# Gate and up products by halves of the input channels, expert weights reloaded piece by piece, and the last block's inner columns taken ahead of the late one-hots

## The reference

```python
h = rms_norm(x, norm2_g)
# 4 groups of 8 experts; every token picks one group and its 2 best experts in it
xb = h_pad[buf_tok].reshape(n_blocks, MOE_BLOCK, D)      # rows gathered by expert
def expert_block(args):
    x_b, e = args
    hid = jax.nn.silu(x_b @ w_gate[e]) * (x_b @ w_up[e])  # 1024 -> 512 channels
    return hid @ w_down[e]                                # 512 -> 1024
y = einsum('tkd,tk->td', y_assign, gates)                 # two results of a token, weighted
x = rms_norm(x + y, final_g)
```

## Time and profile before

| what | value |
| --- | --- |
| median of 3 runs | 965.87 us (964.38 to 966.78) |
| the profiled execution's own time | 967.03 us |
| its span, first to last instruction | 964.9 us |
| PE busy | 857.3 us, 89% of the span |
| DVE busy | 430.1 us, 45% |
| mean granted TensorE clock | 0.948 of full speed |
| HBM read and written | 247.52 MB and 27.08 MB |

### The profile page before, as it was taken

One profiled execution on the slowest core, in us unless ns is written; L12 is line 12 of the kernel. 1 busy time (PEld: TensorE's weight loads), 2 busy tenths in 40 slices (PEclk: granted clock), 3 DMA queues, 4 the chain that ended last, 5 costly groups with the idle time before them and its releaser, 6 DMA issues.

```text
span 964.9 us, 15627 instructions
## 1 busy us (share of the span) xinstructions
PE 857.3 (89%) x5808; PEld 578.9 (60%) x5809; DVE 430.1 (45%) x622; ACT 249.0 (26%) x486; POOL 157.5 (16%) x286
## 2 busy tenths in 40 slices
PE   3989999999779994699999988898889999899965
PEld 2879978778468883555555545453445555455532
DVE  5499979848977434422222221111121222212276
ACT  5214274563745222011111111111011111111112
POOL 4100000000011000222222221111111222121162
PEclk9989999999979995599999999999899999999988
DMA  7444435221183737499999999999999999999454
GB/s 199 121 121 117 155 144 184 61 71 44 32 265 141 303 133 311 176 368 401 393 399 400 399 405 403 413 404 415 399 412 396 391 408 390 400 401 349 159 201 130
DMA packets 80890, 265.75 MB, mean 275 GB/s; under 512 B 18092, under 2 KB 43948, under 8 KB 56280
## 3 DMA queue, kind: packets, MB, share of 16 engines
q1 hardware_dynamic: 63232, 245.10, 66.6%
q0 software_dynamic: 7808, 18.54, 5.5%
q10 hardware_dynamic: 9816, 1.66, 0.9%
HBM read 247.52 MB, written 27.08 MB: 285 GB/s over the span
## 4 chain that ended last, share of the span: by engine, by line
PE 59%; SPq 17%; DMA 11%; DVE 7%; issue 3%; ACT 1%; ACTq 0%; POOL 0%; POOLq 0%; DVEq 0%
SPq L723 17%; PE ps L1203 14%; PE ps L1001 12%; DMA ring<-in_w_up 10%; PE ps L1236 7%; PE ps L1123 7%; PE ps L997 4%; PE ps L1206 2%; PE ps L1194 2%; DVE big L1583 2%; PE ps L1020 1%; PE ps L1215 1%; PE ps L1050 1%; PE ps L1029 1%; PE ps L1266 1%
## 5 line engine op out<-in xcount | busy, mean ns | idle before, releaser
L1206 PE MATMUL ps<-ring,big 128*64 128x256 f32 x896 | 211.5, 395 | 21.5 <-DMA ring<-in_w_up 21.3
L1203 PE MATMUL ps<-ring,big 128*64 128x256 f32 x896 | 214.3, 395 | 4.8 <-DMA ring<-in_w_gate 3.6
L1203 PEld LDWEIGHTS ps<-ring,big 128*64 128x64 f32 x896 | 125.5, 142 | 66.7 <-issue 18.8
L1206 PEld LDWEIGHTS ps<-ring,big 128*64 128x64 f32 x896 | 126.3, 143 | 51.9 <-DMA ring<-in_w_up 29.0
L1829 DVE TENSOR_TENSOR big<-ps,big 64x256 f32<-64x256 f32 x78 | 33.1, 426 | 267.1 <-ACT big L1480 267.0
L1001 PE MATMUL ps<-hT,w_split 128*128 128x512 f32 (+1 forms) x768 | 145.2, 344 | 4.1 <-DVE hT L1539 3.6
L1001 PEld LDWEIGHTS ps<-hT,w_split 128*128 128x128 f32 x768 | 118.0, 190 | 25.6 <-issue 11.3
L1583 DVE SCALAR_TENSOR_TENSOR big<-big,vec 128x783 f32<-128x783 f32 x116 | 119.6, 1031 | 3.0
L1480 ACT ACTIVATE big<-ps 64x256 f32<-64x256 f32 x78 | 29.3, 375 | 292.4 <-PE ps L1206 292.4
L1236 PE MATMUL ps<-ring,big 128*64 128x512 f32 x224 | 103.2, 604 | 0.0
L1237 PE MATMUL ps<-ring,big 128*64 128x512 f32 x224 | 103.2, 604 | 0.0
(11 more groups left out here) (213 smaller groups left out, 1121.8 us busy)
## 6 DMA issues: line engine op xcount, KB each, us to landing
ring<-in_w_gate SPq DMA_DIRECT2D x44, 1024.0 KB, 28.1
ring<-in_w_up SPq DMA_DIRECT2D x44, 1024.0 KB, 29.1
ring<-in_w_down SPq DMA_DIRECT2D x44, 1024.0 KB, 29.2
big<-in_w_gate SPq DMA_DIRECT2D x20, 1024.0 KB, 28.7
big<-in_w_up SPq DMA_DIRECT2D x20, 1024.0 KB, 29.8
big<-in_w_down SPq DMA_DIRECT2D x20, 1024.0 KB, 29.5
w_raw<-in_w_in SPq DMA_DIRECT2D x20, 512.0 KB, 4.0
results<-spare POOLq DMA_DIRECT2D x12, 512.0 KB, 2.9
```

Of the source, the lines that this page charges most:

```text
L1203: pe.matmul(ps[0:BLK, 6 * h, 0:FH], xT[:, k, :], gate_w[s][:, k, fs], start=(k == 0), stop=(k == KD - 1))
L1206: mm = pe.matmul(ps[BLK:2 * BLK, 6 * h + 1, 0:FH], xT[:, k, :], up_w[s][:, k, fs], start=(k == 0), stop=(k == KD - 1))
```

## The change

It has four parts.

1. `gate_up` takes a further argument q, the half of the input channels. A block now runs q = 0 for both halves h of the inner columns, and then q = 1 for both. The number of matmuls and what they sum are as before. A new semaphore, `gu_half`, is raised after q = 0, h = 1.
2. `load_expert` waits on `gu_half` ahead of the first two pieces (gate and up of the first channel half), on `gu_done[1]` ahead of the next two, and on `y_done` ahead of down, as before.
3. In DVE's tail `hidden(last)` stands ahead of the late one-hots. `result(last)` follows these, and all four `with_stored` come behind it.
4. The semaphores of the two norm vectors become one, counted to 16 and 32.

```diff
+            def load_some(e, s, first, end):
+                for l in list(in_order(s))[first:end]:
                     load(e, *l)
 ...
                 end = sp.value_load(table[0:1, bass.ds(e + (2 * E - SLOTS), 1)], min_val=1, max_val=MAXB)
+                sp.wait_ge(gu_half, end)
+                load_some(e, s, 0, 2)
                 sp.wait_ge(gu_done[1], end)
-                load_gate_up(e, s)
+                load_some(e, s, 2, 4)
                 sp.wait_ge(y_done, end)
-                load_down(e, s)
+                load_some(e, s, 4, 6)
...
-            def gate_up(b, s, target, h):
+            def gate_up(s, target, q, h):
 
                 fs = slice(h * FH, (h + 1) * FH)
-                for k in range(KD):
+                for k in range(q * KD // 2, (q + 1) * KD // 2):
                     if h == 0 and k % (KD // 2) == 0:
-                        pe.wait_ge(gate_in[s][k // (KD // 2)], target)
+                        pe.wait_ge(gate_in[s][q], target)
...
-                mm.then_inc(gu_done[h], 1)
+                if q:
+                    mm.then_inc(gu_done[h], 1)
+                elif h:
+                    mm.then_inc(gu_half, 1)
...
-                gate_up(b, s, target, 0)
-                gate_up(b, s, target, 1)
+                for q in range(2):
+                    for h in range(2):
+                        gate_up(s, target, q, h)
...
+            hidden(last)
 
             dve.wait_ge(late_copied, 2)
...
-            with_stored(0)
-            hidden(last)
-            for t in range(1, BY_VECTOR):
+            result(last, 1, pairs + 2, late_y)
+            for t in range(BY_VECTOR):
                 with_stored(t)
-            result(last, 1, pairs + 2, late_y)
```

More of the change, by code:

```diff
@@ L553, in encoder @@
         x_in = [sem(f"x_in{t}") for t in range(NT)]
-        vec_in, small_in, n2_in, fin_in = sem("vec_in"), sem("small_in"), sem("n2_in"), sem("fin_in")
+        vec_in, small_in, norms_in = sem("vec_in"), sem("small_in"), sem("norms_in")
         n1_in = sem("n1_in")
@@ L603, in encoder @@
             [sem(f"{what}{h}") for h in range(2)] for what in ("gu_done", "sg_ready", "hb_ready", "ht_ps", "ht_ready"))
-        pe_passed, pool_passed = sem("pe_passed"), sem("pool_passed")
+        pe_passed, pool_passed, gu_half = sem("pe_passed"), sem("pool_passed"), sem("gu_half")
         taken_in = [sem(f"taken_in{t}") for t in range(NT)]
@@ L662, in _ @@
             sp.dma_start(br[:], bass.AP(router_b.tensor, 0, [[0, P], [1, NR]])).then_inc(small_in, 16)
-            sp.dma_start(n2[:], bass.AP(norm2.tensor, 0, [[0, P], [1, D]])).then_inc(n2_in, 16)
+            sp.dma_start(n2[:], bass.AP(norm2.tensor, 0, [[0, P], [1, D]])).then_inc(norms_in, 16)
             def load_raw(h):
@@ L736, in load_expert @@
                 end = sp.value_load(table[0:1, bass.ds(e + (2 * E - SLOTS), 1)], min_val=1, max_val=MAXB)
+                sp.wait_ge(gu_half, end)
+                load_some(e, s, 0, 2)
                 sp.wait_ge(gu_done[1], end)
-                load_gate_up(e, s)
+                load_some(e, s, 2, 4)
                 sp.wait_ge(y_done, end)
-                load_down(e, s)
+                load_some(e, s, 4, 6)
             sp.wait_ge(wout_done, 1)
             sp.wait_ge(ssa_done, 1)
-            load_gate_up(2, 2)
+            load_some(2, 2, 0, 4)
             pieces = [list(in_order(s)) for s in range(2)]
@@ L764, in _ @@
                         load(e, *l)
-            sp.dma_start(fin_g, bass.AP(final_g.tensor, 0, [[0, P], [1, D]])).then_inc(fin_in, 16)
+            sp.dma_start(fin_g, bass.AP(final_g.tensor, 0, [[0, P], [1, D]])).then_inc(norms_in, 16)
             sp.wait_ge(h2_out, 32 * NT)
             sp.wait_ge(h2t_done, NT)
-            load_down(2, 2)
+            load_some(2, 2, 4, 6)
             sp.wait_ge(table_ready, 1)
@@ L1195, in turn_rows @@
                 mm.then_inc(xt_ps, 1)
-            def gate_up(b, s, target, h):
+            def gate_up(s, target, q, h):
                 fs = slice(h * FH, (h + 1) * FH)
-                for k in range(KD):
+                for k in range(q * KD // 2, (q + 1) * KD // 2):
                     if h == 0 and k % (KD // 2) == 0:
-                        pe.wait_ge(gate_in[s][k // (KD // 2)], target)
+                        pe.wait_ge(gate_in[s][q], target)
                     pe.matmul(ps[0:BLK, 6 * h, 0:FH], xT[:, k, :], gate_w[s][:, k, fs], start=(k == 0), stop=(k == KD - 1))
                     if h == 0 and k % (KD // 2) == 0:
-                        pe.wait_ge(up_in[s][k // (KD // 2)], target)
+                        pe.wait_ge(up_in[s][q], target)
                     mm = pe.matmul(ps[BLK:2 * BLK, 6 * h + 1, 0:FH], xT[:, k, :], up_w[s][:, k, fs],
                                    start=(k == 0), stop=(k == KD - 1))
-                mm.then_inc(gu_done[h], 1)
+                if q:
+                    mm.then_inc(gu_done[h], 1)
+                elif h:
+                    mm.then_inc(gu_half, 1)
             def turn_hidden(b, h):
@@ L1671, in second_norm @@
                 if t == 0:
-                    dve.wait_ge(n2_in, 16)
+                    dve.wait_ge(norms_in, 16)
                 dve.wait_ge(root2, t + 1)
@@ L1895, in last_norm @@
                                                ALU.mult, ALU.mult).then_inc(fin_done, 1)
-            dve.wait_ge(fin_in, 16)
+            dve.wait_ge(norms_in, 32)
             for t in range(NT):
```

## The result

The changed kernel takes 958.12 us (median of 8 runs, 956.84 to 962.36) where the kernel before takes 966.33 us (8 runs, 963.59 to 969.15). The ratio is 0.9921, with a 95% interval from 0.9899 to 0.9944, so it is faster by 0.6 to 1.0%. In a later comparison, with other runs of both, the ratio was 0.9946 (0.9929 to 0.9962). The profiled execution took 958.9 us with a span of 956.8, against 964.9 before: 8.1 us less.

What follows compares the result with a forecast made beforehand. The prediction took the weight stream's start, its last awaited up piece, PE's work after that and the tail to set the end. 3.46 + 1.73 + 4.0 = 9.2 us off 965.87 gave 956.7 us, range 953.0 to 961.0.

Steps and rivals of the forecast that it cites:

- All three gains: Earlier weight stream 3.46 us, work moved ahead of the last up piece 1.73, shorter DVE tail 4.0; chance 0.70.
- the middle term: After PE's last wait for an up piece: 8 pairs less work remain, 1.73 us gained.
- The stream's start: First reload, expert 3's first two pieces: released by gu_half, it and every landing come 3.46 us earlier.
- Behind the last landing: After the last awaited up piece: 8 + 8 pairs remain, not 8 + 16; 1.73 us, perhaps 1.7 of clock.
- The tail: After the last block: earlier results let PE's late products reach tile 2 3.4 to 5.4 us sooner; 4.0 taken.
- The new deadline of the transposes: turn_hidden(0) in every block: the later silu and product, about 1.0 us, stay covered with 0.6 us to spare.
- slower: Rival: turn_hidden(0) becomes a wait in each block, losing 13 us against 9.2 gained; 970 us, chance 0.04.

Runs made afterwards that it cites:

- loops_only: The changed kernel without its tail part (DVE's tail as in the kernel before); 960.39 us, 0.9948 of before.
- order_only: The kernel before with the new order of channel halves; all four gate and up pieces still released by gu_done[1], tail as before; 963.53 us, 0.9980.
- first_only: The changed kernel with the tail of before and gu_half releasing pieces only for expert 3, the first reload; 960.98 us, 0.9946 of before.
- all_but_first: The changed kernel with the tail of before and gu_half releasing pieces for every expert but expert 3; 963.31 us, 0.9978 of before.
- tail_only: The kernel before with the changed DVE tail alone; 963.65 us, 0.9964 of before.
- again: The changed kernel run once more, unaltered, in a later comparison; 959.48 us, 0.9946 of before.
- warm_first: The changed kernel with matmuls of unused result in PE's pauses ahead of the first block; 957.51 us, 0.9911 of before.
- warm_denser: The changed kernel with unused matmuls in PE's pauses before the first block, three behind the gates' products; 957.33 us, 0.9928 of before.

## Why the prediction was right

Forecast were 956.7 us from a median of 965.87, a gain of 9.2 us. Measured were 8.2 us between the medians, 7.6 by the ratio, and 5.2 by the ratio of the second comparison. All three gains exist. The sum was 1 us too high by the profile and 4 us by the second comparison. That it came so near in the profile is in part luck: the middle term came out 1.1 us above its forecast, the other two 0.9 and 1.25 us below.

**The stream's start: right, 3.46 us forecast.** The reload moved by 3.41 us relative to the first block. The agreement with 3.46 is closer than the measure allows, since this distance moved by up to 1.8 us from one execution to another with the clock in the first block. Of the 3.41, 2.54 arrived at the last wait in the profiled pair, because the block began 0.53 us later and the stream took 0.34 longer. In time it is the difference of loops_only and order_only: 0.0032, or 3.1 us. first_only and all_but_first show that it is the start that counts.

**Behind the last landing: right in mechanism, too small in size for this profile.** 1.73 us were forecast, with up to 1.7 of clock on top. Measured are 2.84 us in the changed kernel and 2.9 to 3.1 in all others that have the order (76.0 to 76.2 us instead of 79.09). PE's busy time in the stretch fell by 3.15 us (79.04 to 75.89), and the wait of 0.35 us for a down piece takes some of it back. Of the 3.15, the 8 pairs are 1.73, and the rest goes with the clock: behind the last up piece it is at 1.00 in all eleven profiled executions with the new order, and at 0.50 and 0.58 in before and tail_only (78.83 us). Why it stays up is not shown; the wait ahead of it is shorter, 1.3 us instead of 1.8. In time order_only gives just 1.9 us. That would fit executions of before in which the clock holds too, but no row shows one, and the interval reaches to 3.6 us.
The Trainium skill (TensorE: Matmul & The Clock Gate, "HAM oscillation — how this bites in real kernels"), drawn on in the prediction, describes a kernel in which the work behind each wait for its next weights starts on the low level. Here the clock is at 1.00 behind waits of 1.46 and 1.30 us in order_only, and of 1.29 us in the changed kernel. The waits of that example are given as 3 to 5 us, so these shorter ones don't speak against it.

**The tail: right in mechanism, 4.0 forecast, 2.75 measured.** The start of tile 2 was forecast 11.8 to 13.8 us after the last silu, and it came at 12.62. The term failed in its last step, in which I took 4.0 although 1.7 us of clock might be lost: the clock was at 0.51 behind the pause, as that sentence allowed, and 10.5 us became 12.3. In again, where the clock held, the tail is 3.66 us shorter than before. The 27.68 us of before are themselves one of five executions with that tail, which took 26.18 to 28.33. tail_only has 3.5 us in time.
Of the one-hots I had given 928 to 931.9 on the clock of before, 2.6 to 6.5 us after the last silu. They ended at 924.66, 4.6 after it. Only one of the four instructions was held up (3.12 against 0.96 us), and `result` was not: its product with PSUM input took 0.76 us.

**The new deadline of the transposes: right.** Nothing waits for `hb_ready[0]`, and the block takes 11.99 us as before. The list of PE's waits from 390 us to the end has no L1216:

```profile
PE ps L1204 <- DMA ring<-in_w_up: 23.5, 17, 1.9
PE ps L1204 <- DMA big<-in_w_up: 7.1, 5, 1.9
PE ps L1268 <- DVE x L1890: 2.9, 1, 2.9
...
PE ps L1201 <- DMA ring<-in_w_gate: 2.5, 4, 1.0
```

The rival *slower* was priced from this chain, and the rows leave it no place.

## What to carry to other kernels

Where a stream of transfers runs full for most of a stage, its first transfer is what matters: find the idle time of the DMA engines ahead of it, and shorten what that one transfer waits for, by finer release or by a faster first block. Releasing the later ones early gave nothing here. Behind the last landing, order the work so that what needs the last piece is least. And when a wait is removed from a tail, look at once for what the moved work now stands in front of: taking out the first tile ahead of the other additions was worth another 2 us by the profile.

## What the runs showed of the hardware

- The stream of 1 MB pieces took 435.6 to 436.1 us from the first reload to the last up piece that PE waited for in ten of thirteen profiled executions, and 436.5 to 437.5 in the other three, with PE's order, waits and clock differing among them.
- The granted clock fell to 0.51 behind a pause of 2.85 us in one execution and stayed at 1.00 behind one of 3.39 us, at the same place of the same kernel. In other kernels it fell there behind 2.83 us (tail_only) and stayed behind 3.25 and 3.40 (warm_first, warm_denser).
- A DVE copy with a single input in SBUF is slowed too while POOL adds: L1825 (64x1024) took 2.67 us in the changed kernel and 0.69 in loops_only, where it began as one of POOL's additions ended.
- The first stage, which is the same code in all of them, ended up to 2.8 us apart: the first block began at 400.47 us in before and at 403.28 in tail_only.
